# A modulation block, a norm weight and three tables moved to later places in a decoder layer

## The reference

```python
mod = (silu(c) @ w_ada + b_ada)                 # six vectors of 1024: sh_m, sc_m, g_m, sh_f, sc_f, g_f
h = rms_norm(x, g) * (1 + sc_m) + sh_m
z = h @ w_in                                    # sections sc_x, sc_b, sc_c, u, v, gate_a, gate_b
y_a = sc_b * causal_dwconv3(sc_c * sc_x, conv_w)
v = layer_norm(gelu(v), ln_v_g)                 # ln_v_g: the value-norm weights
y_b = gelu(u) * (tril(w_spatial) @ v + b_spatial)
x = x + g_m * ((sigmoid(gate_a) * y_a + sigmoid(gate_b) * y_b) @ w_out)
h = rms_norm(x, g2) * (1 + sc_f) + sh_f
x = x + g_f * experts(h)                        # top 4 of 32, clamped SwiGLU
out = rms_norm(x, final_g)
```

## Time and profile before

| what | value |
|---|---|
| median of three runs | 1154.68 us |
| lowest, highest | 1153.91, 1155.73 us |
| span of the profiled execution | 1151.8 us |
| TensorE busy | 957.4 us (83%) |
| VectorE busy | 357.2 us (31%) |
| ScalarE busy | 243.4 us (21%) |
| DMA moved | 467.30 MB, mean 406 GB/s |

### The profile page before, as it was taken

How to read it: one execution, slowest core, us unless ns; L and a number is a source line. 1 busy time by engine, 2 the same in 40 slices (tenths; PEclk the granted TensorE clock), 3 DMA queues, 4 the chain that set the end, 5 groups by cost and what they waited for, 6 DMA issues and landing times.

```text
span 1151.8 us, 23787 instructions
## 1 busy us (share of the span) xinstructions
PE 957.4 (83%) x9707; PEld 505.7 (44%) x9708; DVE 357.2 (31%) x801; ACT 243.4 (21%) x365; POOL 8.6 (1%) x28
## 2 busy tenths in 40 slices
PE   7989999998986976987888888888876876876784
PEld 5789999743442321433333333443321322331331
DVE  3689796571221111212121121221211211211112
ACT  3435444530110110111111111110100100100112
POOL 0010000000000000000000000000000000000000
PEclk9989999999998998999998999999998998898997
DMA  9999788999999999999999999999999999999996
GB/s 358 377 340 357 293 311 318 412 400 428 427 425 427 426 426 427 426 426 425 425 426 427 427 426 426 427 426 427 426 426 426 427 426 427 427 426 426 427 424 273
DMA packets 62413, 467.30 MB, mean 406 GB/s; under 512 B 5180, under 2 KB 6516, under 8 KB 27572
## 3 DMA queue, kind: packets, MB, share of 16 engines
q1 hardware_dynamic: 62144, 466.65, 98.1%
q10 hardware_dynamic: 244, 0.29, 0.1%
HBM read 465.87 MB, written 1.05 MB: 405 GB/s over the span
## 4 chain that ended last, share of the span: by engine, by line
PE 42%; DMA 40%; SPq 8%; DVE 6%; issue 4%; ACT 1%; PEldq 0%; DVEq 0%; ACTq 0%
PE B L1405 22%; DMA trio<-in_w_down_dram 21%; DMA W<-in_w_down_dram 14%; PE B L1093 10%; SPq L411 4%; PE B L1424 3%; DMA W<-in_w_gate_up_dram 3%; SPq L413 3%; PE B L1414 2%; DVE wl L743 2%; DMA spare<-in_w_ada_dram 2%; PE B L1351 2%; PE B L1357 1%; DMA raw<-in_w_in_dram 1%; DVE spare L793 1%
## 5 line engine op out<-in xcount | busy, mean ns | idle before, releaser
L1405 PE MATMUL B<-W,trio 128*32 128x512 f32 (+1 forms) x4784 | 451.4, 522 | 85.6 <-DMA W<-in_w_gate_up_dram 77.3
L1405 PEld LDWEIGHTS B<-W,trio 128*32 128x32 f32 x4784 | 163.3, 112 | 347.7 <-issue 168.2
L661 ACT ACTIVATE EW<-EW 128x256 f32<-128x256 f32 x46 | 19.2, 416 | 683.1 <-DVE EW L1023 683.1
L1023 DVE TENSOR_SCALAR EW<-B 128x256 f32<-128x256 f32 x46 | 19.5, 425 | 463.9 <-PE B L1405 463.9
L1093 PE MATMUL B<-hh,wh 128*128 128x256 f32 x384 | 110.4, 288 | 4.2 <-DVE wl L743 4.2
L1093 PE MATMUL B<-hl,wh 128*128 128x256 f32 x384 | 109.8, 286 | 0.0
L1093 PE MATMUL B<-hh,wl 128*128 128x256 f32 x384 | 109.7, 286 | 0.0
L1414 PE MATMUL B<-b_gu,trio 128*32 128x512 f32 x368 | 50.4, 616 | 66.6 <-issue 55.2
L743 DVE TENSOR_TENSOR wl<-raw,wh 128x2048 fp32r<-128x2048 f32 (+1 forms) x36 | 73.3, 2074 | 18.2 <-ACT wh L556 17.7
L556 ACT ACTIVATE wh<-raw 128x2048 fp32r<-128x2048 f32 (+1 forms) x36 | 60.2, 1719 | 84.0 <-DMA raw<-in_w_in_dram 53.8
L1093 PEld LDWEIGHTS B<-hh,wh 128*128 128x128 f32 x384 | 74.9, 195 | 4.6 <-issue 4.0
(11 more groups left out here) (245 smaller groups left out, 689.8 us busy)
## 6 DMA issues: line engine op xcount, KB each, us to landing
W<-in_w_gate_up_dram SPq DMA_DIRECT2D x112, 2048.0 KB, 35.2
W<-in_w_down_dram SPq DMA_DIRECT2D x48, 2048.0 KB, 38.4
spare<-in_w_gate_up_dram SPq DMA_DIRECT2D x16, 2048.0 KB, 28.6
trio<-in_w_down_dram SPq DMA_DIRECT2D x15, 2048.0 KB, 41.0
raw<-in_w_in_dram SPq DMA_DIRECT2D x12, 2048.0 KB, 9.5
raw<-in_w_ada_dram SPq DMA_DIRECT2D x9, 2048.0 KB, 9.6
raw<-in_w_in_dram SPq DMA_DIRECT2D x4, 1024.0 KB, 15.7
raw<-in_w_out_dram SPq DMA_DIRECT2D x2, 2048.0 KB, 8.9
```

The costliest lines, as they stand in the source:

```text
L661: A(sg, gs, ACT.Sigmoid, scale=ALPHA).then_inc(sig_ready, 1)
L1023: V.tensor_scalar(halves(gs), paired(GU[:, 0:QC]), LIMIT, None, ALU.min).then_inc(gmin_ready, 1)
L1405: t = M(o, src[:, k % KQ, CAP * (k // KQ):CAP * (k // KQ) + CAP], w, start=(first and k == 0), stop=(k == KT - 1))
```

## The change

The order of the units of the first half is now SC_C, modulation block 0, SC_X, SC_B, block 1, GATE_A, block 2, U, block 3, GATE_B. It was SC_C, block 0, SC_X, block 1, SC_B, block 2, GATE_A, block 3, U, GATE_B. The tables are asked for behind SC_B and no longer behind SC_X. In the first half VectorE weighs block n in section n (1 to 3), a section later than before, and the sum over the partitions on TensorE stands behind U and no longer behind GATE_A; the bias is added behind GATE_B. The value-norm weights are applied (`value_weight`) behind the second bank of SC_B. The wait for the spatial biases moves into section U. The second half (h = 1) is as it was.

```diff
--- before.py
+++ after.py
@@ -63,7 +63,9 @@
     for h in range(NH):
         for i, s in enumerate(SECTIONS):
             units.append(("in", s, h))
-            if i < 4:
+            if h == 0 and i in (0, 2, 3, 4):
+                units.append(("ada", 1, max(i - 1, 0)))
+            if h > 0 and i < 4:
                 units.append(("ada", 1 + h, i))
     units += [("out", 0, h) for h in range(NH)]
     PARTS = 2
@@ -383,12 +385,12 @@
                     sp.dma_start(dst[:, 4:8, :], src[:, 4:8, :]).then_inc(landed(n)[0], 16)
                 else:
                     sp.dma_start(dst, src).then_inc(landed(n)[0], 16)
-                if n == split_units[3]:
+                if n == split_units[4]:
                     sp.wait_ge(modT_done, 4)
                     sp.dma_start(ws_nat, w_spatial[0].rearrange("g t s -> t g s")).then_inc(s_ws, 16)
                     sp.dma_start(lng, ln_v_g[0].partition_broadcast(P)).then_inc(s_lng, 16)
                     sp.dma_start(bs_all, b_spatial[0].partition_broadcast(P)).then_inc(s_bs, 16)
-                if n == split_units[3]:
+                if n == split_units[4]:
                     for j in range(4):
                         sp.dma_start(mod[32 * j:32 * j + 32, 1:3, :], ba[j][1:3].partition_broadcast(32)).then_inc(s_bada_rest, 16)
                 if n == split_units[5]:
@@ -806,11 +808,15 @@
             V.tensor_scalar(stat[:, VVAR:VVAR + TA], stat[:, VSS:VSS + TA], 1.0 / D, EPS, ALU.mult, ALU.add).then_inc(v_var, 1)
             dve.wait_ge(v_std, 1)
             step(V.reciprocal(stat[:, VRST:VRST + TA], stat[:, VSTD:VSTD + TA]))
-            dve.wait_ge(s_lng, 16)
             for a in range(TA):
                 step(V.tensor_scalar(HV[:, a, :], HV[:, a, :], stat[:, NMU + a:NMU + a + 1],
                                      stat[:, VRST + a:VRST + a + 1], ALU.add, ALU.mult))
-                V.tensor_tensor(HV[:, a, :], HV[:, a, :], lng, ALU.mult).then_inc(v_ready, 1)
+
+            def value_weight():
+
+                dve.wait_ge(s_lng, 16)
+                for a in range(TA):
+                    V.tensor_tensor(HV[:, a, :], HV[:, a, :], lng, ALU.mult).then_inc(v_ready, 1)
 
             def tiles(bank):
                 return bank[:, :].rearrange("p (t n) -> p t n", n=T)
@@ -821,7 +827,6 @@
                 t2 = slice(4 * h + 2 * b, 4 * h + 2 * b + 2)
                 V.tensor_tensor(ml[:, t2, :], accB[:, 2 * b:2 * b + 2, :], mh[:, t2, :].bitcast(f32), ALU.subtract).then_inc(m_ready, 1)
 
-            dve.wait_ge(s_bs, 16)
             for h in range(NH):
                 for n, s in enumerate(SECTIONS):
                     for b in range(2):
@@ -858,6 +863,7 @@
                             V.tensor_tensor(accB[:, two, :], accB[:, two, :], tiles(sig), ALU.mult).then_inc(sec_dve, 1)
                         elif s == U_:
                             c = 2 * h + b
+                            dve.wait_ge(s_bs, 16)
                             dve.wait_ge(sp_done, c + 1)
                             bias = bs_all[:, 4 * h + 2 * b:4 * h + 2 * b + 2, :].unsqueeze(2).broadcast_to([P, 2, TA, P])
                             V.tensor_tensor(stmp.rearrange("p (t a n) -> p t a n", t=2, a=TA),
@@ -870,11 +876,15 @@
                             V.tensor_tensor(accC[:, two, :], accC[:, two, :], tiles(sig), ALU.mult).then_inc(sec_dve, 1)
                             dve.wait_ge(sec_dve, dve_bank(h, s, b))
                             V.tensor_tensor(accB[:, two, :], accB[:, two, :], accC[:, two, :], ALU.add).then_inc(m_sum, 1)
-                        if b == 0 and n < 3:
+                        if b == 0 and h == 0 and 1 <= n < 4:
+                            weigh(1, n)
+                        if b == 1 and h == 0 and s == SC_B:
+                            value_weight()
+                        if b == 0 and h > 0 and n < 3:
                             weigh(1 + h, n + 1)
                         if b == 0 and s == GATE_B and h + 1 < NH:
                             weigh(2 + h, 0)
-                    if s == U_:
+                    if s == (GATE_B if h == 0 else U_):
                         add_bias(1 + h)
                 m_low(h, 1)
             split_low(len(split_units) - 1)
@@ -1252,7 +1262,7 @@
                         turn_spatial()
                     if s == U_:
                         spatial(2 * h + 1)
-                    if s == GATE_A:
+                    if s == (U_ if h == 0 else GATE_A):
                         sum_weighed(1 + h)
 
             def spread(dst, i, j, signal):
```

## The result

The changed kernel takes 1157.47 us (median of five runs, 1157.39 to 1159.71), the kernel before 1154.12 us (five runs, 1153.63 to 1155.73). The ratio is 1.0031 with a 95% interval from 1.0017 to 1.0044: 3.4 us or 0.3% slower, beyond the 0.2% that counts as no change. The range 1152.0 to 1159.0 holds it. The forecast of 1155.8 lies 1.7 us under it, and the forecast's own range (1153.0 to 1157.0) ends 0.5 us under it. Its likeliest case, a change within 0.2%, did not come; the case "slower" had 20%.

What follows compares the result with a forecast made beforehand. Expert stage bound by its weights, asked for when the mixer ends; VectorE full from 68 to 109 us. GATE_B, with a 6.1 us stop and 2.3 us of clock, starts 1.1 us later: 1154.68 + 1.1 = 1155.8 us, range 1152.0 to 1159.0.

Steps and rivals of the forecast that it cites:

- likeliest case: Whole kernel: time within 0.2% (2.3 us) of the kernel before, given 68%.
- the case "slower": Whole kernel: slower than the kernel before by more than 0.2% (2.3 us), given 20%.
- The old stop and its clock: TensorE before SC_B: the 3.82 us stop goes, with its 2.68 us lost to half clock; SC_B starts at 75.71.
- The chain on VectorE: VectorE's work up to the value weights: 22.18 us from GATE_A's first high half at 82.7, ready at 104.85.
- The new stop: TensorE before the first spatial products: waits from 98.75 to 104.85 for the value weights, 6.1 us.
- The clock behind it: TensorE after the new idleness: lower clock, 1.3 to 2.7 us lost, 2.3 taken.
- The hand-over to the end: Mixer to expert stage: the 1.1 us later start of GATE_B comes out at the kernel's end as 1.1 us.
- A: TensorE before GATE_B: old stop goes, none comes; GATE_B 7.3 us earlier, 1147.4 us; 5%.
- B: TensorE after the new stop: clock stays up; GATE_B 3.0 us earlier, 1151.6 us; 7%.
- C: GATE_A's block lands late, at 86.55; GATE_B starts at 127.4, 1161.9 us; 17%.
- D: Expert stage: swallows the mixer's shift, 1154.7 us; 5%.

Runs made afterwards that it cites:

- r4: The kernel before, unaltered, profiled a third time: 1153.29 us.
- e2: The kernel before with only the value-norm weights moved behind the second bank of SC_B: 1161.25 us, ratio 1.0059.
- e1: The changed kernel with the value-norm weights applied behind the second bank of SC_X and not of SC_B: 1153.47 us, ratio 0.999.
- e3: The changed kernel with the value-norm weights applied right behind the norm, as before the change: 1152.32 us, ratio 0.9983.
- e6: The changed kernel with the small tables asked for behind GATE_B's block and not behind GATE_A's: 1155.95 us, ratio 1.001.
- e5: The changed kernel with 56 unused transposes on TensorE between GATE_A and the first spatial products of the first half: 1155.56 us, ratio 1.0013.
- e4: The kernel of e3 with third and fourth weighings a section later, column sum behind GATE_B, small tables behind GATE_B's block: 1148.32 us, ratio 0.9947.
- e7: The kernel of e3 with the four tables asked for behind SC_X, as before the change: 1152.12 us, ratio 0.998.

## Why the prediction was right in its mechanism and short in its size

**The old stop and its clock.** Right in what it forecast. SC_B starts at 75.34 at full clock, and two sections follow unbroken. (The 75.7 predicted is the end of the turning as the row shows it, 74.68 + 1.03; the next matmul starts 0.8 us behind the turning's start, before that end.) But the prediction took the slow matmuls behind the old stop for the price that GATE_B's start paid. Two rows speak against it: in r4 the clock was back earlier, and GATE_B started at 120.08 all the same. TensorE's timeline before, then r4's, with r4's stretch:

```profile
109.17 0.39 PE L1093 MATMUL B<-hh,wh 128*128 128x256 f32 x1 [0.34 <-DVE wl L743]
```

```profile
109.09 0.38 PE L1093 MATMUL B<-hh,wh 128*128 128x256 f32 x1 [0.45 <-DVE wl L743]
```

```profile
84.00:86.00 2.00, 2.00 (x19) 2.00 (x19) 1.93 (x3) 0.00 (x0) 0.00 (x0) 1.00 1.10 203
```

In both, the second half of U's product waits for its low half, and GATE_B starts 10.99 us later. So in the kernel before, too, VectorE set the start of GATE_B. The slow matmuls behind the old stop had slack there. The sum for the changed kernel did not use that price, except as a measure for the new stop's clock.

**The chain on VectorE.** SC_X's block, asked for at 46.90 together with SC_B's, was used at 56.35 and not at 54.9, and the norm ended 0.6 us later than the prediction has it. It cost nothing, since VectorE still waited 1.11 us for GATE_A's block.

**The new stop.** Right in its place, its releaser and its reason, too small in its length: predicted 6.1 us, with 5 to 7 as the sign of being right, measured 7.2, and 7.6 and 7.8 in the repetitions. e2 shows that the place of the value weights makes it, e1 and e3 that it goes with them. The value weights ended it at 105.84, not 104.85. Half of the missing microsecond is the landing of GATE_A's block, 81.27 and not 80.8; the other half is the wait for U's block, 0.36 us, which the sum did not have, and 0.1 us of smaller gaps. The prediction has no term for U's block at all. It let the small tables stand behind GATE_A's block only as a load on the transfers and did not count them in the SyncE queue, where they held back the modulation block, which then came right ahead of U's. e6 took both waits away and gave back 1.5 us.

**The clock behind it.** Right that it falls. 2.3 us was taken, 2.49 measured, 1.8 to 3.1 in three executions. e5 shows it as the price of the stop and not of something that stands beside it. The Trainium skill's rule ("TensorE: Matmul & The Clock Gate", section "HAM oscillation — how this bites in real kernels": bursts between waits start slow, at half of the slow time lost) would have put the forecast 0.6 us higher and nearer, because the prediction put it on the old stop's 5.75 us of slow time. The traces agree with the half: by the granted clock of the stretches the slow time here was some 4.7 us, and 6.1 and 3.1 us in the repetitions, with 2.5, 3.1 and 1.8 us lost. What varies is how long the slow time lasts, and nothing here tells that in advance.

**The hand-over to the end.** The second size that was off. The prediction let 1.1 us of the mixer come out as 1.1 us. The mixer gave 2.3 us, 2.8 over three profiles, and the spans 3.7, the medians 3.4. The shift of the mixer is passed on in full (it is 2.31 us still when the first expert block is asked for in the loop, 252.29 against 249.98), and what comes on top, 0.8 us in the mean of three, lies in the expert stage and its end. 0.3 us of it is the slow scatter of one profile of three. The rest is the time from GATE_B's start to the last down projection: 1019.8 to 1020.0 us in the three profiles before, 1020.2 to 1020.5 in the three of the changed kernel, and up to 1021.8 in the experiments (e5), which have the same stage. Whether the change or the execution sets those 0.5 us, three profiles a side don't tell; that stays open.

**The rivals.** A (no new stop) needed what e4 has: the value weights early, and a weighing fewer ahead of U's split. It was priced at 7.3 us for GATE_B, and e4 gained 6.7 at the next section. B did not come. C did not come as it was put, a landing of GATE_A's block from 82 us on with 86.55 as its case: the block was used at 81.27 (82.30 and 80.65 in the repetitions). A late landing cost 0.5 us and the one of U's block, which C does not name, 0.4. (C's 127.4 takes 2.7 us for the clock; with the sum's own 2.3 it is 127.0.) D did not come. **What was luck:** the time lies above the forecast's own range, and GATE_B's 122.46 above its 118.4 to 122.3. The stated range holds the time through the room that was left for C, while the excess came from elsewhere, half of it from the expert stage, for which the sum had no term. The chances were off: with a forecast of +1.1, an edge at +2.3 and an unknown expert stage, "slower" deserved more than 20%.

## What to carry to other kernels

When an engine is full, a transfer that comes earlier only moves the wait: count the engine's own work ahead of each result that another engine waits for, and make first what is wanted first. Here 2.4 us of multiplications, moved behind the split of a later section, cost 6.5 us in the old order (e2), while the rest of the change without them gained 2.4 us (e3) and with two weighings moved away 6.4 (e4). A stop of TensorE is to be priced with its clock: 7.2 us of waiting brought 2 to 3 us of slow matmuls behind it. A shift of 0.2% or less needs several profiles, since the stage bound by transfers varied by 2 us between kernels that have it alike (1019.8 to 1021.8 us).

## What the runs showed of the hardware that was not expected

**Small requests hold the queue.** In the changed kernel SyncE needed from 63.32 to 81.91 us for the twelve requests of the small tables, with the four tables, a modulation block and GATE_A's block ahead of them; in e6, asked for from 97.36 on behind one block, they took 8.9 us, and in the kernel before, behind GATE_A's block, 9.9 (77.50 to 87.36). That the transfers queued ahead make them slow is what these orders suggest; no run parts it from other causes. The large block right behind them was asked for at 81.96 and not at 73.94, and the one behind that, U's, was used at 96.28 and not at 91.80, though it was asked for at nearly the same time (82.42 and 82.17).

**GpSimd and VectorE side by side.** Before, a selection on GpSimd ran beside VectorE's subtraction of 58.57. GpSimd's timeline before, and after, where VectorE was idle at that time:

```profile
59.90 1.86 POOL L500 TENSOR_SCALAR_AFFINE_SELECT tmp<-tmp 128x128 bf16<-128x128 bf16 x1
```

```profile
65.06 0.29 POOL L502 TENSOR_SCALAR_AFFINE_SELECT tmp<-tmp 128x128 bf16<-128x128 bf16 x1
```

The same instruction takes 1.86 us beside the subtraction and 0.29 us by itself. VectorE's two subtractions took 5.34 us beside it and take 4.49 alone, by VectorE's timeline of the changed kernel:

```profile
58.37 4.49 DVE L745 TENSOR_TENSOR wl<-raw,wh 128x2048 fp32r<-128x2048 f32 x2 [2.91 <-ACT wh L558]
```

This agrees with the Trainium skill, "SBUF — State Buffer", section "SBUF: two separate sides": a VectorE instruction with two inputs in SBUF and a GpSimd instruction that reads SBUF hold the shared port in turn, and one waits for the whole of the other. The rows agree in that both sides take longer; they don't show which instruction waited for which. e7 is the changed kernel's VectorE order with the tables early again, so that the two run side by side, and it has 1.86 and 5.30 us again.
